# Expert value products with the table as the held operand: sums come out by feature, and the last norm runs over partitions

## What is computed

```python
# PEER: 16384 experts, 8 heads, 16 experts chosen for each head and token
z    = x_normed @ u.T                     # [256, 16384], only the chosen entries count
act  = gelu(z) * gate                     # gate is zero where an expert was not chosen
x    = x + act @ v                        # v: [16384, 2048]
# last norm
out  = x * rsqrt(mean(x * x, axis=-1) + 1e-6) * norm_final_g
```

## Time and profile before

| | |
|---|---|
| median of 3 runs | 3221.04 us (3218.38 to 3222.54) |
| the profiled execution | 3221.12 us, its span 3219.2 us |
| granted TensorE clock, mean | 0.998 of full |
| PE busy | 3190.0 us (99%), 25285 matmuls |
| DVE, ACT busy | 2253.7 us (70%), 1686.2 us (52%) |
| DMA | 569.94 MB, mean 177 GB/s, 16 engines about 50% busy |

### The profile page before, as it was taken

The page is one execution under the profiler, slowest core; times in us unless marked ns, Lnnn a source line. Parts: engine busy times, 40 slices in busy tenths (PEclk is TensorE's granted clock), DMA queues, the critical chain, the costliest instruction groups (busy, mean ns, idle before and its releaser), DMA issues.

```text
span 3219.2 us, 63022 instructions
## 1 busy us (share of the span) xinstructions
PE 3190.0 (99%) x25285; PEld 3031.9 (94%) x25285; DVE 2253.7 (70%) x3778; ACT 1686.2 (52%) x2283; POOL 33.4 (1%) x46
## 2 busy tenths in 40 slices
PE   8999999999999999999999999999999999999998
PEld 8999999999999999999999999998899889988887
DVE  8767667655566786566679987765677557788765
ACT  5444455767775556555544444444444444444444
POOL 4000000000000000000000000000000000000000
PEclk9999999999999999999999999999999999999999
DMA  5444445444445544545454555555555555555554
GB/s 186 163 150 168 147 162 189 158 158 167 164 162 185 197 164 160 192 165 188 161 186 177 187 186 183 180 188 196 184 183 183 196 192 185 179 180 181 184 208 157
DMA packets 99095, 569.94 MB, mean 177 GB/s; under 512 B 9456, under 2 KB 30320, under 8 KB 31600
## 3 DMA queue, kind: packets, MB, share of 16 engines
q1 hardware_dynamic: 98928, 567.58, 49.8%
HBM read 565.45 MB, written 2.10 MB: 176 GB/s over the span
## 4 chain that ended last, share of the span: by engine, by line
PE 90%; DVE 7%; DVEq 1%; ACT 1%; issue 1%; DMA 0%; POOL 0%; ACTq 0%; POOLq 0%; SPq 0%
PE bank L583 20%; PE bank L584 20%; PE bank L585 20%; PE bank L1104 7%; PE bank L1106 7%; PE bank L1105 7%; DVE wl L1642 2%; PE bank L1029 1%; PE bank L737 1%; PE bank L940 0%; PE bank L686 0%; PE bank L815 0%; PE bank L814 0%; PE bank L972 0%; ACT wh L1138 0%
## 5 line engine op out<-in xcount | busy, mean ns | idle before, releaser
L584 PE MATMUL bank<-hl,wh 128*128 128x256 f32 x5616 | 1558.1, 277 | 0.0
L1642 DVE TENSOR_TENSOR wl<-raw,wh 128x1024 fp32r<-128x1024 f32 x1052 | 1259.9, 1227 | 422.9 <-ACT wh L1138 415.5
L583 PE MATMUL bank<-hh,wh 128*128 128x256 f32 x5488 | 1541.8, 281 | 2.8 <-DVE wl L1642 1.7
L585 PE MATMUL bank<-hh,wl 128*128 128x256 f32 x5488 | 1520.5, 277 | 0.0
L1138 ACT ACTIVATE wh<-raw 128x1024 fp32r<-128x1024 f32 x1052 | 1051.6, 1050 | 270.4 <-DMA raw<-w_in_a 124.2
L584 PEld LDWEIGHTS bank<-hl,wh 128*128 128x128 f32 x5616 | 1057.4, 188 | 1.9 <-issue 1.7
L583 PEld LDWEIGHTS bank<-hh,wh 128*128 128x128 f32 x5488 | 1034.7, 189 | 7.4 <-issue 2.5
L585 PEld LDWEIGHTS bank<-hh,wl 128*128 128x128 f32 x5488 | 1030.8, 188 | 0.0
L1104 PE MATMUL bank<-wh,ah 128*128 128x512 f32 x1024 | 401.9, 392 | 0.0
L1106 PE MATMUL bank<-wl,ah 128*128 128x512 f32 x1024 | 399.0, 390 | 0.0
L1105 PE MATMUL bank<-wh,al 128*128 128x512 f32 x1024 | 398.4, 389 | 0.0
(11 more groups left out here) (412 smaller groups left out, 3165.0 us busy)
## 6 DMA issues: line engine op xcount, KB each, us to landing
raw<-peer_u SPq DMA_DIRECT2D x128, 1024.0 KB, 4.9
raw<-peer_v SPq DMA_DIRECT2D x128, 1024.0 KB, 4.9
raw<-w_in_c SPq DMA_DIRECT2D x64, 1024.0 KB, 4.9
raw<-w_in_a SPq DMA_DIRECT2D x63, 1024.0 KB, 4.9
raw<-w_kv SPq DMA_DIRECT2D x32, 1024.0 KB, 4.9
raw<-w_in_b SPq DMA_DIRECT2D x32, 1024.0 KB, 4.9
raw<-w_out_a SPq DMA_DIRECT2D x16, 1024.0 KB, 5.0
raw<-w_out_b SPq DMA_DIRECT2D x16, 1024.0 KB, 5.0
```

What stands on the lines that cost most here:

```text
L583: eng.matmul(out, h_[:, k, :], high[:, k, :], start=(k == 0), stop=False)
L584: eng.matmul(out, h_[:, k, :], low[:, k, :], start=False, stop=False)
L585: last = eng.matmul(out, low_rows(c, k), high[:, k, :], start=False, stop=(k == KC - 1))
L1642: eng.tensor_tensor(low_half_out(c, half), raw_half(c, half), high_half(c, half).bitcast(F32), ALU.subtract).then_inc(lo_ready, 1)
```

## The change

- In a V unit the table is held in the array and the activations move: for each group j and each of its eight 128-feature chunks three products of 256 columns, 48 in a unit in place of 24 (`value_products`). A bank holds two feature chunks by 256 tokens.
- The sums have features on partitions like the stream, so `stream_turn` and its copies in U0 go, and `add_experts` adds to `xT` as it stands.
- In the last half block the last two units are done bank by bank, so that the banks are finished one after the other (`last_units_by_bank`). It waits for the activations and low parts of both units before it begins.
- The last norm sums over partitions: squares of each pair of chunks (`xsq`), added up on DVE (`add_squares`), summed by a product with ones (`final_sum`), root on ACT and reciprocal on DVE of 128x256 values. The weights come from `prm`, one value per partition, and ACT multiplies them in (14 of 16 chunks) while PE still works. The last multiplication by the inverse root is all on DVE, in four pieces, and each piece is stored when it is ready, two by SP and two by ACT.
- `fin` and its load go. `DENSE`, `FIRST` and `TURNS` are new names for 256, 0 and 32.

```diff
+            def value_products(bank, k, c, j, n, opens, closes):
+                for e in range(2):
+                    w_h, w_l = wh[k % RAW][:, j * FH + 2 * n + e, :], low_rows(k, j * FH + 2 * n + e)
+                    out_ = bank[:, e * T:e * T + DENSE]
+                    a_h, a_l = ah[c % 2][:, j, :], al[c % 2][:, j, :]
+                    eng.matmul(out_, w_h, a_h, start=opens and e == 0, stop=False)
+                    eng.matmul(out_, w_h, a_l, start=False, stop=False)
+                    last = eng.matmul(out_, w_l, a_h, start=False, stop=closes and e == 1)
+                return last
...
-                                k = j * FH + h * FH // 2
-                                w_h = wh[k0_ % RAW][:, k:k + FH // 2, :].rearrange("p k n -> p (k n)")
-                                w_l = low_rows(k0_, k, FH // 2)
-                                a_h, a_l = ah[c % 2][:, j, t * P:(t + 1) * P], al[c % 2][:, j, t * P:(t + 1) * P]
-                                eng.matmul(bank[:, :], a_h, w_h, start=first, stop=False)
-                                eng.matmul(bank[:, :], a_l, w_h, start=False, stop=False)
-                                last = eng.matmul(bank[:, :], a_h, w_l, start=False, stop=final)
+                                last = value_products(B[(SUM_BANK[q] + n) % SUM_BANKS], k0_, c, j, n, first, final)
...
+                def last_units_by_bank(b, q):
+                    eng.wait_ge(s["al_ready"], (q + 1) * (BJ // 2))
+                    eng.wait_ge(lo_ready, 2 * ALL_UNITS)
+                    for n in range(FH // 2):
+                        for c in (BJ // 2 - 2, BJ // 2 - 1):
+                            for j in range(2):
+                                last = value_products(B[(SUM_BANK[q] + n) % SUM_BANKS], BASE[f"V{b}"] + BJ // 2 + c, c, j, n, False,
+                                                      c == BJ // 2 - 1 and j == 1)
...
+            def final_sum():
+                eng.wait_ge(s["xsq_summed"], 1)
+                eng.matmul(B[7][:, 0:T], ones[:, :], xsq[:, 0, 0:T], start=True, stop=False)
+                eng.wait_ge(s["xsq_ready"], KC // 2)
+                for e in range(2):
+                    last = eng.matmul(B[7][:, 0:T], ones[:, :], xsq[:, KC // 2 - 1, e * T:(e + 1) * T], start=False, stop=(e == 1))
...
-                        if b == 0 and isinstance(i, int) and i == 0:
-                            stream_turn(c)
...
-                        eng.wait_ge(s["xt_done"], c + 1)
-                        eng.activation(chunk(xT, 2 * c, 2), B[6 + c % 2][:, :], ACT.Copy).then_inc(s["xt_ready"], 1)
...
+                for n in range(FH // 2):
+                    g = f * FH // 2 + n
+                    eng.wait_ge(s["x_added"], 8 * BLOCKS - 7 + g)
+                    eng.activation(xsq[:, g, :], chunk(xT, 2 * g, 2), ACT.Square).then_inc(s["xsq_ready"], 1)
+                    if g < KC // 2 - 1:
+                        eng.drain()
+                        for c in (2 * g, 2 * g + 1):
+                            last = eng.activation(xT[:, c, :], xT[:, c, :], ACT.Copy, scale=col("fin", c))
...
+                    if b == BLOCKS - 1 and BJ - 6 <= n < BJ - 3:
+                        add_squares(n - BJ + 7)
...
+            for n in range(FH // 2):
+                add_experts(BLOCKS - 1, 1, n, n + 1)
+                if n > 0:
+                    add_squares(FH // 2 + n - 1)
+            eng.tensor_tensor(xsq[:, 0, 0:T], xsq[:, 0, 0:T], xsq[:, 0, T:2 * T], ALU.add).then_inc(s["xsq_summed"], 1)
+            eng.wait_ge(s["frs_ready"], 1)
+            eng.reciprocal(rstd[:, :], rstd[:, :])
...
+            for g in range(4):
...
+                if g == 3:
+                    for c in (KC - 2, KC - 1):
+                        eng.scalar_tensor_tensor(out=xT[:, c, :], in0=xT[:, c, :], scalar=col("fin", c), in1=rstd[:, :],
+                                                 op0=ALU.mult, op1=ALU.mult)
...
+                eng.tensor_tensor(xT[:, chunks, :], xT[:, chunks, :], rstd[:, :].unsqueeze(1).broadcast_to([P, n, T]),
+                                  ALU.mult).then_inc(s["y_ready"], 1)
```

More of the change, by code:

```diff
@@ L53 @@
 TG = T // BJ
+DENSE = T
+FIRST = T - DENSE
+TURNS = DENSE // TG
 G_SCALE = 2.0 ** 14
@@ L500, in _, with block_of @@
             row("Q", w_q, KC)
-            def block_of(name, table, b, first=0, end=BJ // PER_PAIR):
-                with eng.Fori(first, end) as i:
+            def block_of(name, table, b):
+                with eng.Fori(0, BJ // PER_PAIR) as i:
                     for c in range(PER_PAIR):
                         load(i, BASE[f"{name}{b}"] + c, one(table, i * PER_PAIR + (b * BJ + c)))
-            for name, b in PEER_ORDER[:-1]:
+            for name, b in PEER_ORDER:
                 block_of(name, peer_u if name == "U" else peer_v, b)
-            block_of("V", peer_v, BLOCKS - 1, 0, 2)
-            eng.wait_ge(mm_done, 2 * BASE["V3"])
-            eng.dma_start(fin, fin_h).then_inc(sQ["fin_in"], 16)
-            block_of("V", peer_v, BLOCKS - 1, 2)
-            for n in range(2 * NT):
-                t, f = n // 2, 1 - n % 2
-                eng.wait_ge(sQ["y_weighed"] if f == 1 else sQ["y_scaled"], t + 1)
-                eng.dma_start(out[:, t, f * D // 2:(f + 1) * D // 2], y[:, t, f * D // 2:(f + 1) * D // 2]).then_inc(sQ["stored"], 16)
-            eng.wait_ge(sQ["stored"], 16 * 2 * NT)
+            for g in (0, 2):
+                eng.wait_ge(sQ["y_ready"], g + 1)
+                eng.dma_start(out[:, 4 * g:4 * g + 4, :], xT[:, 4 * g:4 * g + 4, :]).then_inc(sQ["stored"], 16)
+            eng.wait_ge(sQ["stored"], 16 * 4)
         @block.gpsimd
@@ L1031, in spread @@
                 last.then_inc(s["g_done"], 1)
-            def stream_turn(c):
-                eng.wait_ge(hl_ready, SPLIT_AT["Q"] + FH)
-                if past_zero(c - 1):
-                    eng.wait_ge(s["xt_ready"], c - 1)
-                for n in range(2):
-                    for t in range(NT):
-                        a = (n * NT + t) * P
-                        last = eng.transpose(B[6 + c % 2][:, a:a + P], xT[:, 2 * c + n, t * P:(t + 1) * P], ident[:, :])
-                last.then_inc(s["xt_done"], 1)
             def dots(b, i, c):
@@ L1082, in half @@
                     q = 2 * b + f
-                    for c in range(BJ // 2):
+                    ends = b == BLOCKS - 1 and f == 1
+                    for c in range(BJ // 2 - 2 if ends else BJ // 2):
                         k0_ = BASE[f"V{b}"] + f * BJ // 2 + c
-                        if b == BLOCKS - 2:
+                        if b == BLOCKS - 2 and f * BJ // 2 + c < TURNS:
                             spread(BLOCKS - 1, f * 2, c)
@@ L1092, in half @@
                                 eng.wait_ge(s["x_added"], 4 * q if f == 0 and b < BLOCKS - 1 else 4 * q - 4)
-                            for n in range(2 * NT):
-                                t, h = n // 2, n % 2
-                                bank = B[(SUM_BANK[q] + n) % SUM_BANKS]
+                            for n in range(FH // 2):
                                 if first and n == 1 and f == 0:
@@ L1122, in _ @@
             v_block(3)
+            final_sum()
         @block.scalar
@@ L2377, in gate_turns, with add_experts @@
                         gate_rows(b + 1, 0, 1)
-            def add_experts(b, f):
+            def add_experts(b, f, first=0, end=FH // 2):
                 q = 2 * b + f
-                for n in range(2 * NT):
-                    t, h = n // 2, n % 2
+                for n in range(first, end):
                     if n < 3:
@@ L2417, in v_turns @@
                         act_low(b + 1, 0, 0)
-                    if n == BJ - 1 or n == BJ // 2 - 1 and not gating:
+                    if n == BJ - 1 and b < BLOCKS - 1 or n == BJ // 2 - 1 and not gating:
                         add_experts(b, n // (BJ // 2))
-                    if b == BLOCKS - 1 and n == BJ // 2 + 2:
-                        eng.wait_ge(s["fin_in"], 16)
-                        for t in range(NT):
-                            weigh_stream(0, t)
+                    if b == BLOCKS - 1 and BJ - 6 <= n < BJ - 3:
+                        add_squares(n - BJ + 7)
             for h in range(PEER_HEADS):
```

124 lines of the change are left out of this document (55 added, 69 removed).

## The result

The changed kernel takes **3274.2 us** (median of 4 runs, 3272.9 to 3277.2) against 3220.6 beside it (4 runs): a ratio of 1.0168, 95% interval 1.0150 to 1.0186. The forecast of 3225.8 and its range up to 3233.0 were too low. The profiled execution has a span of 3275.2 against 3219.2 us, 56.0 more.

The account below looks back on a forecast made before the run. PE, streaming products back to back, was taken as the bound (90% of the chain). V units 0, spreads -0.6, U0 -0.4, last two units +2.2 and tail +3.5 made +4.7 on 3221.1: 3225.8 us, range 3222.0 to 3233.0.

Parts of the forecast that it names:

- V units: V blocks on PE: 48 products of 256 columns take 5.44 us, as 24 of 512 did; 0 us.
- Rival 1: V blocks step at 0.118 us: 6.9 us a block, 3232.7 with one, 3246.5 with all three; chance 0.15.
- U0: Expert choice, bound by DVE: only the one turn ahead of DVE's wait gives time back, -0.4 us.
- -3.5: U0's bound and rival 3: all eight stream_turn on PE come back, 3.5 us instead of 0.4, 3222.7; chance 0.05.
- Spreads and the last two units: V2's units with a spread save 0.6 us; PE's wait before V3's last two units helps make +2.2.
- The 0.4 for long steps behind it: Last 96 products behind the wait in V3 go at 0.118 us a step, adding 0.4 us.
- The tail: From the last product's record end to the span's end: 13.8 us against 10.3 before, +3.5 us.
- Rival 2: Clock falls in the waits before the last units or the sum with ones: 1.5 or 1.3 us; chance 0.13.
- ACT was in time in V3: Rival 4: ACT late with unit 23's activations in V3, margin 0.7 us; about 1 us, 3226.8; chance 0.05.
- Back-to-back issue gap: Skill's fixed 2.5 ns per matmul: 3072 more would cost 7.7 us, result 3233.5; judged against the rows, chance 0.02.

Follow-up runs that it names:

- e12: e9 with one pace() product of 64 columns ahead of the first product of each V block: 3225.5 us, ratio 1.0012.
- e5: Changed kernel with the final norm's weights out of prm and 32 unused columns ahead of ah, so each tile starts where it did before: 3265.5 us (1.0142).
- e14: Kernel before the change with pace() ahead of the first and fifth unit of each stage C turn and OC's first unit: 3216.1 us (0.9980).
- e13: e12 with pace() also ahead of the first and fifth unit of each stage C turn and OC's first unit: 3218.3 us (0.9987).
- e3: Changed kernel with 16 unused columns (64 bytes per partition) behind prm alone: 3282.0 us (1.0183).
- e15: e13 with only the last unit, not the last two, done bank by bank at the end of V3: 3219.3 us (0.9989).
- e9: e5 with 16 unused columns ahead of ah in place of 32, so ah and al start at a multiple of 128 bytes: 3239.8 us (1.0055).
- e4: Kernel before the change with 16 unused columns behind prm and 16 more ahead of ah: 3249.8 us (1.0092).
- e1: Changed kernel with 16 unused columns ahead of ah and al: 3249.2 us (1.0098).
- e10: Kernel before plus rows of 48 products at varied operand starts behind its last product; 256 columns, held 64 and moving 64: 0.1200 us a step.
- e2: Changed kernel with 16 unused columns behind prm and 16 more ahead of ah: 3296.0 us (1.0231).
- e7: Changed kernel with the value products as before the change, holding activations and moving 512 columns of the table: 3257.3 us.

## Why the prediction was wrong

**V units: this step failed.** "0, because the time goes by columns" holds in e12, where 48 products of 256 take what 24 of 512 took. It does not hold by itself. The 256-column pair of starts that the change makes (ah and al at 64, wh and wl at 64) takes 0.1200. The term that I had at 0 was 10.3 us in V0, 10.2 in V1 and some 15.8 in V2 and V3 (16.9 less the 1.1 that spreads and wait cost in e12), 36 in all. The range ended at one block with the longest step that I had seen, 0.118. Rival 1 named the kind of cost and where to see it, and its reason against (a V block begins without a bubble) was no reason: V0 went long without one. It was priced for three blocks of four and at 0.0045 a step; it was 0.0066 in all of V0 and V1, and I gave it 0.15.

**What I left out of the sum: the places.** The 16 columns of prm stood in the diff, and I gave them no term at all. They moved every tile behind prm by 64 bytes, and OC started 15.6 us later; with all tiles back (e5) 1.1 earlier than before. The ladder in medians: 3274.2; all other tiles back 3265.5; ah and al at a multiple of 128 3239.8; the rhythm set 3225.5. By the first step V2 and V3 lost again part of what the early stages gave (118.7 to 120.0 ns).

**U0.** Forecast -0.4. From product 12,000 to 15,360 the difference to before changes by +1.2 in after, -1.3 in e5, 0.0 in e12, and the kernel before has 240 products at 0.1178 there. So -3.5 isn't seen, and the -0.4 can't be told from the rhythm.

**Spreads and the last two units.** -0.6 + 2.2 = 1.6 forecast, 1.1 measured in e12 and against e14 in e13. The wait was right, 1.7. The 0.4 for long steps behind it didn't come: in e12 the steps there are 0.1133. In e3 the step behind the same wait was even the shorter one, 0.1133 against 0.1178 ahead of it.

**The tail.** 13.8 forecast, 14.0 after, so +3.6 for +3.5. In e12, e13 and e15 it was 14.5, 15.0 and 14.0; the first two have the clock's fall in them (next paragraph).

**The other rivals.** In the changed kernel the clock stayed at 1.00 behind both waits. Rival 2 did come in others of these kernels, behind the second wait, ahead of the sum with ones: the six records of that sum took 1.56 us after and in e15 at 1.00, 2.05 in e12 at 0.72 and 2.57 in e13 at 0.58. So it cost 0.5 and 1.0 us where 1.3 was priced; PE's idle time ahead of the sum, 1.9 us, was the same in all four. ACT was in time in V3: apart from the wait there is no gap over 0.3 us in the block. With the steps made equal, the change by its own work cost 3.6 us by the medians of e12 and before and 2.2 by those of e13 and e14, where 4.7 was forecast. So the rest of the sum was right to some 1 to 2.5 us, on the high side, and the miss is the length of a step. That e12 has 3225.5, the forecast to 0.3 us, is in part luck: the early stages alone stand 1.1 us below to 2.6 above before at the start of OC in e5, e9 and e12, which have them in the same places.

The Trainium skill, page TensorE: Matmul & The Clock Gate, section Back-to-back issue gap, gives N / 2.4 plus about 2.5 ns as the gap of an isolated matmul and says itself that the formula does not give the spacing in a stream of weight loads and matmuls, for which the prediction took it. The runs show no fixed part: 113.3 and 226.7 ns for 256 and 512 columns, twice to 0.1 ns, 1.0625 times the columns at 2.4 GHz in the best case. And they show 117.8 or 120.0 for the same 256 columns, for which it has no term.

## What to carry to other kernels

Read the step of back-to-back products in each stage, from starts in the timeline, before and after any change, also where nothing was changed: two unused pads of 64 bytes cost 29 us here (e4) with no work added. When an operand changes from held to moving, look at where both start within 128 bytes, and try a pad before judging the change. Run a kernel more than once before a single profile is believed: e1 has 17 us between its runs. If the same operands show two lengths of step, a short product ahead of the stretch is worth a run; here 16 of them made the old kernel 0.2% faster.

## What the runs showed of the hardware

- The step of fp32r products depends on where both operands start within 128 bytes (e5 against e9, and the rows of e10), and not on that alone (U in e2 and e3, V in e4 and e7). 256 columns: 113.3 to 120.0 ns; 512 columns: 226.7 to 237.0, means over a unit, the highest in V2, whose units stand behind a spread.
- A pair of starts that differ by 64 bytes has two rhythms, 113.3 and 117.8 ns for 256 columns. A stretch without a break stays in the one it begins in, over 192 products in stage A and 1536 in V0; behind a wait of 1.7 us it changed once (e3, 117.8 to 113.3). Which one it is goes with what stands ahead of the stretch (e9 against e12). That the places of other tiles act through the products ahead (osq_a and ones in stage A, the spreads' tiles in e2) is argued and not shown; in e2 the spreads' tiles have the same place within 128 bytes as before.
- At 2.4 GHz, which the granted clock of 1.00 is, 113.3 and 120.0 ns are 272 and 288 cycles, 17 and 18 times 16, where 256 columns are 16 times 16; 117.8 is 282.7 in the mean. What in the machine makes them so was not shown. Nor was it settled what sets the rhythm: pace() gave the short one in V0, V1, C and OC and for 0 against 64 in the bench, and not for 64 against 0 where each product opened its bank. Moving single tiles of the early stages wasn't tried.
